# An earlier root, a later compressed branch and moved skip products in a kernel of two transformer blocks

## The chip, the cores and the metric

The kernel runs on one core of a Trainium2 chip (trn2). The metric is the device time of one execution in microseconds (us). The engines are TensorE (PE; PEld are its weight loads), VectorE (DVE), ScalarE (ACT), GpSimd (POOL) and SyncE (SP), which issues the loads of the weights.

## The reference

The input is a sequence of 256 tokens with 1024 features in fp32. The first block has four layers, each a mixer, an MLP with a squared relu and a gate:

```python
for i in range(DEPTH):                # 4
    h = rmsnorm(x, g[0]); kind = i % 3
    ...                               # 0: diff_attention, 1: nsa_attention, 2: forgetting_attention
    x = x + rmsnorm(y, g[1])
    y = sqrelu_mlp(rmsnorm(x, g[2]), mlp_w1[i], mlp_w2[i])
    x = x + rmsnorm(y, g[3])
    x = x + sigmoid(x @ ple_gate_w[i]) * (p[i] @ ple_w[i])
```

Layer 0 is a difference of two softmaxes per head, with a bias that depends on the distance of query and key. Its factor comes from four vectors:

```python
lam_full = exp(sum(lf[0] * lf[1])) - exp(sum(lf[2] * lf[3])) + lam_init
a = pr[:, :, 0] - lam_full * pr[:, :, 1]
```

Layer 1 (`nsa_attention`) has three branches per head, mixed by gates: a selected branch and a window branch on all 256 keys, and a compressed branch on 15 averaged blocks of keys, whose masked softmax gives 0 in a row where no block is visible yet:

```python
p_c = masked_softmax(s_c, m_c)        # 15 blocks; m_c: block wholly in the past
o_c = einsum('bgrqn,bngd->bqgrd', p_c, vc)
return gc[..., 0:1] * o_c + gc[..., 1:2] * o_s + gc[..., 2:3] * o_w
```

The second block has two layers. Each has, beside a latent attention, a state-space branch that ends in

```python
y = ssd_chunked_scan(xh, dt, a, bm, cm) + xh * d_skip[:, None]
```

## The kernel before, in words

The kernel is written as one program per engine, with semaphores between them. An engine runs its own program strictly in the order in which it is written, so a waiting instruction holds up all that stands behind it on that engine. No scheduler changes that order.

**Weights.** SP loads weights in pieces of 128x2048 into one of four slots. ACT rounds each to fp32r (`act_hi`, L441), DVE subtracts to get the rest (`dve_lo`, L451), and PE multiplies three times (L468, L469, L470). Most of PE's work is this. Each `act_hi` and `dve_lo` is placed by hand between the other steps of its engine.

**The start of layer 0** (`act_start`, `dve_start`, `act_da`, `pe_da`). ACT squares the input in four pieces (L632), POOL adds (L608) and DVE finishes the sums (`dve_last_squares`, L620 and L622). PE sums them over the partitions (L628). ACT takes the root (`act_std`, L636, which loads a table of functions first), DVE inverts it (L648), PE spreads it over the partitions (L596), and DVE copies it to `st` (L643). `dve_lam` (L1701, L1703) makes the two sums for the factor `lam_full`, `act_lam` (L1673) their exponentials. In the meantime POOL issues the load of 2 MB of bias rows (L1560). `pe_flip` (L1571) reverses these in two halves of four banks each, and `act_flip` (L1577) copies the banks back. The second half uses the banks of the first, so it waits for those copies. `act_exp_ready` (L1807) loads the table for the exponentials ahead of the attention.

**The second attention** (`act_nsa`, `dve_nsa` and their PE program, layer 1). A loop over 16 pairs j runs scores (L1460), turns of the probabilities (`turn`, L2037) and `values` (L2046 to L2048) on PE. DVE adds the bias and sums the rows (`scaled`: L1379, L1384) and takes up the output (`out`: L1390 to L1415). `values(j)` waits for `out(j-1)`. Weights still come in the first seven pairs. The compressed branch lies in pairs 7 to 15. Its scores are on PE at j=7. At j=8 DVE clears and fills `vbd` (L2269 memset, L2307 copies), adds the biases (L2312) and takes the maxima. At j=9 it normalizes, with a mask (L2326). Then PE turns the probabilities and multiplies them (`block_turned` L2023, `block_values` L2028) at j=10 to 15, and DVE adds the results (`added`, L2276).

**The scan** (second block, both layers) runs over four groups g. DVE makes `bounded` (L2843), `inputs` (L2859, L2861 and the skip products L2864) and `weighted` (L2849). PE's products inside a chunk (L2524) wait for `weighted`, and the next strip of weights in `pe_T` (L468) overwrites what `bounded` reads.

Of the kernel before, what the change touches and what calls it, by code (L numbers as in the profile page):

```python
# [16 lines left out]
P = 128  # L17
D = 1024
S = 256
# [119 lines left out]
def build(nc, d, out, stop=None):  # L139
    ctx = ExitStack()  # L140
    with ctx:
# [152 lines left out]
        s_ca = sem("s_ca")  # L294
        s_stl = sem("s_stl")
# [1071 lines left out]
        def dve_attention(E, n, kind, table, wide=64, strips=None, deep=16, tail=None, middle=None):  # L1367
# [53 lines left out]
            for j in range(n):  # L1421
# [4 lines left out]
                if j < deep and j + 1 < n and (strips is not None or j + 2 < n):  # L1426
                    scaled(j + 1)
                if j >= deep and j + 2 < n:
                    scaled(j + 2)
                if j:  # L1430
                    out(j - 1)
# [129 lines left out]

        def pe_flip(E, half):

            if half:
                E.eng.wait_ge(s_mixa, E.next(s_mixa))
            else:
                E.eng.wait_ge(s_const, E.next(s_const, n_const))
                E.eng.wait_ge(s_rows, E.next(s_rows, 16))
            for b in range(4):
                at = 8 * half + 2 * b  # L1570
                nc.tensor.matmul(ps[:, 2 + b, :], flip[:, :], bias[:, at:at + 2, :].rearrange("p h k -> p (h k)"), start=True, stop=True).then_inc(s_tp, E.adds(s_tp))  # L1571

        def act_flip(E, half):
            for b in range(4):
# [66 lines left out]
        def act_start(E, gcol):  # L1641
# [21 lines left out]
            act_hi_half(E, 1)  # L1663
            E.eng.wait_ge(s_tp, E.next(s_tp))
            nc.scalar.activation(g2[:, 0:n2], ps[:, 3, 0:n2], ACT.Copy)
            for b in range(4):
                act_square(E, b, xT[:, 2 * b:2 * b + 2, :], s_qd)
            act_hi(E)
            act_hi(E)
# [5 lines left out]
        def dve_start(E, gcol):  # L1675
# [18 lines left out]
            dve_lo(E)  # L1694
# [53 lines left out]
        def pe_da(E, layer):  # L1748
# [11 lines left out]
            E.eng.wait_ge(s_st, E.next(s_st))  # L1760
# [23 lines left out]
        def act_da(E, layer):  # L1784
# [5 lines left out]
            act_std(E, DC, 3)  # L1790
# [4 lines left out]
            if layer == 0:  # L1795
                act_flip(E, 0)
# [154 lines left out]
        vcs = view(ar, 12544, [P, 4, 64])  # L1951
# [27 lines left out]
        def pe_nsa(E):  # L1979
# [90 lines left out]
            for j in range(16):  # L2070
# [6 lines left out]
                if j in (0, 2, 4, 5, 6):  # L2077
                    if j == 4:
                        E.eng.wait_ge(s_kv, 1)
                    elif j:  # L2080
                        evicted({2: "q1", 5: "q3", 6: "kwin"}[j])
                    blk = pe_block(E, S, DC)
                    pe_strip(E, "v" if j == 6 else "q", 7, 0, blk)
# [8 lines left out]
                if j in (0, 2, 4, 5, 6):  # L2092
                    pe_strip(E, "v" if j == 6 else "q", 7, 1, blk, s_km if j == 5 else s_mm)
                elif j == 15:
                    E.eng.wait_ge(s_ca, 3)
                    for b in range(2):
                        pe_turn_bank(E, b, orow)
# [8 lines left out]
                if j == 10:  # L2106
                    E.eng.wait_ge(s_cp, 1)
                    block_turned(0)
                elif j == 11:
                    E.eng.wait_ge(s_cc, 1)  # L2110
                    E.eng.wait_ge(s_vb, 1)
                    block_values(0)
                elif j == 12:
                    E.eng.wait_ge(s_ca, 1)
                    block_values(1)
                elif j == 13:
                    E.eng.wait_ge(s_ca, 2)
                    block_turned(1)
                elif j == 14:
                    E.eng.wait_ge(s_cc, 2)  # L2120
                    block_values(0)
                elif j == 15:
                    block_values(1)
            values(15)
            E.skip(s_kd, 3)
# [34 lines left out]
        def act_nsa(E):  # L2160
# [39 lines left out]
            def between(j):  # L2200
# [16 lines left out]
                elif j in (10, 13):  # L2217
                    E.eng.wait_ge(s_ct, {10: 1, 13: 2}[j])
# [4 lines left out]
            act_turn(E)  # L2223

# [5 lines left out]
        def dve_nsa(E):  # L2230
# [48 lines left out]
            def between(j):  # L2279
# [10 lines left out]
                elif j == 3:  # L2290
# [5 lines left out]
                    nc.vector.tensor_copy(vcs[0:NCMP], ps[0:NCMP, 7, S:].rearrange("p (g n) -> p g n", g=4)).then_inc(s_kv, 1)  # L2296
                if 0 < j < 8:
                    dve_lo(E)
                if j == 5:
                    dve_rooted(E, 7)  # L2300
                elif j == 7:
                    nc.vector.memset(pc[:, :, :, NCMP:], 0.0)
                    nc.vector.memset(pc[:, 0:2, :, 7:NCMP], NEG)
                elif j == 8:
                    step(nc.vector.memset, vbd, 0.0)
                    for h in range(4):
                        last = nc.vector.tensor_copy(vbd[32 * h:32 * h + NCMP, :, h, :], vcs[0:NCMP])  # L2307
                    last.then_inc(s_vb, 1)
# [9 lines left out]
                elif j == 9:  # L2318
# [5 lines left out]
                    for q in range(NT):  # L2324
                        x = pc[:, 2 * q:2 * q + 2, :, 0:NCMP]
                        last = nc.vector.tensor_tensor(x, x, cmaskv[:, q, 0:NCMP].unsqueeze(1).unsqueeze(1).to_broadcast([P, 2, 8, NCMP]), ALU.mult)  # L2326
                    last.then_inc(s_d, E.adds(s_d))
                    E.eng.wait_ge(s_d, E.sofar(s_d))
                    nc.vector.tensor_tensor(p15, p15, csm.unsqueeze(3).to_broadcast([P, 4, 8, NCMP]), ALU.mult).then_inc(s_cp, 1)
                elif j in (11, 12, 14, 15):  # L2330
                    added({11: 0, 12: 1, 14: 2, 15: 3}[j])
            dve_attention(E, 16, "nsa", True, strips=between, deep=8)
# [451 lines left out]
        def dve_ssd(E, layer):  # L2784
# [72 lines left out]
            def inputs(g):  # L2857
# [3 lines left out]
                nc.vector.tensor_tensor(xdw[:, :, :], xdt[:, 0], col(2, g), ALU.mult).then_inc(s_xd, 1)  # L2861
                for q in range(NT):
# [6 lines left out]
            for g in range(4):  # L2869
                bounded(g, 0)  # L2870
                E.eng.wait_ge(s_xs, xs0 + 2 * g + 2)
                if g:
                    gated(g - 1, 1)
                    inputs(g)
                    dve_lo(E)
# [3 lines left out]
                else:  # L2879
                    inputs(0)  # L2880
                    weighted(0, 0)
                    dve_lo(E)
                    bounded(0, 1)
# [557 lines left out]
        def _(eng):  # L3441
            E = Track(eng)
            pool_start(E)
            for layer in range(DEPTH):
                pool_added(E, 3)
                pool_added(E, 3)
# [23 lines left out]
        def _(eng):  # L3470
# [3 lines left out]
            act_lam(E)  # L3474
# [19 lines left out]
        def _(eng):  # L3494
            E = Track(eng)
            dve_start(E, g1(0, 0))
            dve_lam(E)
            for layer in range(DEPTH):
                if layer % 3 == 0:
                    lamL[0] = layer // 3  # L3500
                    dve_rstd(E)
                    dve_score_root(E)
                    dve_lo(E)
                    dve_spread(E, 3)
                    dve_strip(E, "k", 0, 1)
                    dve_lo(E)
                    if layer == 0:
# [45 lines left out]
```

## Time and profile before

| | |
|---|---|
| median of 3 runs | 2962.04 us (2955.81 to 2965.88) |
| the profiled execution | 2954.48 us, span 2952.5 us |
| PE busy | 2902.1 us, 98% of the span |
| DVE busy, ACT busy | 2144.8 us, 1532.8 us |
| chain that ended last | PE 88%, DVE 7%, ACT 4% |
| mean granted TensorE clock | 0.989 |

Times in the timelines are us from the start of the span. A row of waits names the waiting engine and line, what it waited for, and the sum, number and longest of the waits. The granted clock is the share of full speed that TensorE was given: 1.00 is 2.4 GHz, near 0.5 is 1.2 GHz.

### The profile page before, as it was taken

To read this page: it belongs to the slowest core of one execution; us is meant where nothing else is said; L and a number is where in the kernel's file an instruction comes from. 1 tells how busy PE (TensorE), PEld (TensorE's weight loads), DVE (VectorE), ACT (ScalarE), POOL (GpSimd) and SP (SyncE) were. 2 spreads that over 40 slices of the span, in tenths; PEclk is the share of its full clock that TensorE was granted. 3 is DMA by queue.
4 is the path that set the end of the run, shared out by engine and by line. 5 is a ranking of instruction groups with operands and counts; after the bars stand their busy time and mean duration, and the time that the engine had idled before them with its cause. 6 is when DMAs were issued, how large, how long until landed. Compare 5 with 4: busy or idle time off the path is not lost.

```text
span 2952.5 us, 44382 instructions
## 1 busy us (share of the span) xinstructions
PE 2902.1 (98%) x18654; PEld 2612.4 (88%) x18654; DVE 2144.8 (73%) x2568; ACT 1532.8 (52%) x2081; POOL 50.6 (2%) x38
## 2 busy tenths in 40 slices
PE   8999998999999999999999999999999999999999
PEld 7888997888988899888988989998888898999988
DVE  5777776676757776776877886658778779765776
ACT  5643565544654356644544845645444466455543
POOL 0000000000000000000100000000000000000000
PEclk9999998999999999999999999999999999999999
DMA  7355451465545654465565544535546544443553
GB/s 241 126 183 198 142 170 55 143 203 175 158 140 172 200 164 140 154 204 192 179 196 159 172 128 148 157 115 191 194 159 210 179 157 137 149 137 125 185 186 114
DMA packets 383191, 482.46 MB, mean 163 GB/s; under 512 B 33201, under 2 KB 330335, under 8 KB 382992
## 3 DMA queue, kind: packets, MB, share of 16 engines
q1 hardware_dynamic: 381832, 477.22, 50.1%
q8 instruction: 148, 2.42, 0.4%
q0 software_dynamic: 560, 2.13, 0.2%
q14 instruction: 51, 0.42, 0.0%
q10 hardware_dynamic: 600, 0.27, 0.0%
HBM read 478.47 MB, written 1.08 MB: 162 GB/s over the span
## 4 chain that ended last, share of the span: by engine, by line
PE 88%; DVE 7%; ACT 4%; issue 2%; POOL 0%; DMA 0%; ACTq 0%; DVEq 0%
PE ps L468 18%; PE ps L470 17%; PE ps L469 17%; PE ps L510 17%; PE ps L514 9%; DVE wl L451 2%; ACT wh L441 2%; PE ps L1460 1%; PE ps L2524 1%; PE ps L781 1%; PE ps L1265 0%; DVE ar L1379 0%; PE ps L2952 0%; PE ps L548 0%; DVE sm L1384 0%
## 5 line engine op out<-in xcount | busy, mean ns | idle before, releaser
L451 DVE TENSOR_TENSOR wl<-raw,wh 128x2048 fp32r<-128x2048 f32 (+1 forms) x462 | 1036.1, 2246 | 352.4 <-ACT wh L441 352.1
L441 ACT ACTIVATE wh<-raw 128x2048 fp32r<-128x2048 f32 (+1 forms) x462 | 860.0, 1874 | 436.0 <-PE ps L510 215.8
L510 PE MATMUL ps<-ahl,wh 128*128 128x512 f32 x2176 | 562.0, 393 | 0.1
L468 PE MATMUL ps<-ahl,wh 128*128 128x256 f32 x1848 | 534.4, 289 | 4.0 <-DVE ar L2843 2.8
L469 PE MATMUL ps<-ahl,wh 128*128 128x256 f32 x1848 | 525.6, 284 | 0.0
L470 PE MATMUL ps<-ahl,wl 128*128 128x256 f32 x1848 | 525.6, 284 | 0.0
L510 PEld LDWEIGHTS ps<-ahl,wh 128*128 128x128 f32 x2176 | 390.5, 189 | 69.3 <-issue 1.3
L468 PEld LDWEIGHTS ps<-ahl,wh 128*128 128x128 f32 x1848 | 357.4, 193 | 12.1 <-issue 5.5
L468 PE MATMUL ps<-wh,ar_r 128*128 128x512 f32 (+1 forms) x944 | 365.0, 387 | 1.2 <-DVE ar_r L1163 1.2
L470 PE MATMUL ps<-wh,ar_r 128*128 128x512 f32 (+1 forms) x944 | 363.8, 385 | 0.0
L469 PE MATMUL ps<-wl,ar_r 128*128 128x512 f32 (+1 forms) x944 | 363.8, 385 | 0.0
L469 PEld LDWEIGHTS ps<-ahl,wh 128*128 128x128 f32 x1848 | 357.5, 193 | 0.3 <-issue 0.2
L470 PEld LDWEIGHTS ps<-ahl,wl 128*128 128x128 f32 x1848 | 357.1, 193 | 0.0
L514 PEld LDWEIGHTS ps<-ahl,wl 128*128 128x128 f32 x2176 | 297.0, 190 | 21.4
L514 PE MATMUL ps<-ahl,wl 128*128 128x256 f32 x2176 | 304.3, 282 | 0.0
L893 ACT ACTIVATE ar_r<-ar 128x512 fp32r<-128x512 f32 x64 | 40.2, 631 | 346.7 <-DVE ar L909 346.7
L468 PEld LDWEIGHTS ps<-wh,ar_r 128*128 128x128 f32 (+1 forms) x944 | 175.4, 186 | 38.7 <-DVE ar_r L1163 2.4
L470 PEld LDWEIGHTS ps<-wh,ar_r 128*128 128x128 f32 (+1 forms) x944 | 175.4, 186 | 36.2
L469 PEld LDWEIGHTS ps<-wl,ar_r 128*128 128x128 f32 (+1 forms) x944 | 175.5, 186 | 35.7
L468 PE MATMUL ps<-wh,ahl 128*128 128x512 f32 (+2 forms) x496 | 171.7, 346 | 2.8 <-issue 1.8
L470 PE MATMUL ps<-wh,ahl 128*128 128x512 f32 (+2 forms) x496 | 168.0, 339 | 0.0
L469 PE MATMUL ps<-wl,ahl 128*128 128x512 f32 (+2 forms) x496 | 168.0, 339 | 0.0
(431 smaller groups left out, 3862.3 us busy)
## 6 DMA issues: line engine op xcount, KB each, us to landing
raw<-in_ffn_w SPq DMA_DIRECT2D x264, 512.0 KB, 4.5
raw<-in_mlp_w SPq DMA_DIRECT2D x256, 512.0 KB, 4.4
raw<-in_w_in SPq DMA_DIRECT2D x124, 512.0 KB, 4.6
raw<-in_da_w_in SPq DMA_DIRECT2D x48, 512.0 KB, 5.0
raw<-in_ple_gate_w SPq DMA_DIRECT2D x32, 512.0 KB, 4.3
raw<-in_w_ssd_out SPq DMA_DIRECT2D x32, 512.0 KB, 4.4
raw<-in_fox_w_in SPq DMA_DIRECT2D x24, 512.0 KB, 4.8
raw<-in_nsa_w_in SPq DMA_DIRECT2D x20, 512.0 KB, 4.9
```

The lines of the kernel that those rows point to most:

```text
L441: nc.scalar.activation(wh[:, slot, 0:sizes[n]], raw[:, slot, 0:sizes[n]], ACT.Copy).then_inc(s_hi, E.adds(s_hi))
L451: nc.vector.tensor_tensor(wl[:, slot, 0:sizes[n]], raw[:, slot, 0:sizes[n]], wh[:, slot, 0:sizes[n]].bitcast(F32), ALU.subtract).then_inc( ...
L468: nc.tensor.matmul(o, wa, xa, start=start, stop=False)
L469: nc.tensor.matmul(o, wa, xb, start=False, stop=False)
L470: return nc.tensor.matmul(o, wb, xa, start=False, stop=stop)
L510: last = nc.tensor.matmul(o, a[:, k, c], ahl[:, k].rearrange("p a t -> p (a t)"), start=k == 0, stop=k == DC - 1)
L514: nc.tensor.matmul(o[:, 0:S], b[:, k, c], ah[:, k], start=False, stop=False)
L781: last = nc.tensor.transpose(o, orow[:, q, c * P:(c + 1) * P], ident[:, :])
L893: nc.scalar.activation(hh[:, u % 3], rr[:, u % 2], ACT.Square).then_inc(s_hh, E.adds(s_hh))
L1460: return nc.tensor.matmul(o, qk[lo, j % 8, 0, qs], keys_of(j)[lo, keys], start=not fox, stop=True)
L2524: last = nc.tensor.matmul(ps[:, 5 + q, 64 * h:64 * h + 64], ee[:, q, h, :], xdt[:, q, h, :], start=True, stop=True)
```

## The change

It has three independent places.

**First block.** ACT's root stands before the last of the first roundings, and DVE's sums come ahead of a rounding. The exponentials for `lam_full` move on ACT from the start to just before the flips. `pe_flip` takes the banks in the order 0, 2, 3, 1, and only bank 1 of the numbering (the fourth taken) waits for `st`.

```diff
 act_start:
+            for b in range(3):
+                act_square(E, b, xT[:, 2 * b:2 * b + 2, :], s_qd)
             E.eng.wait_ge(s_tp, E.next(s_tp))
             nc.scalar.activation(g2[:, 0:n2], ps[:, 3, 0:n2], ACT.Copy)
-            for b in range(4):
-                act_square(E, b, xT[:, 2 * b:2 * b + 2, :], s_qd)
+            act_square(E, 3, xT[:, 6:8, :], s_qd)
             act_hi(E)
+            act_std(E, DC, 3)
             act_hi(E)
 dve_start:
-            dve_lo(E)
             dve_last_squares(E)
             dve_lo(E)
 pe_flip:
-            for b in range(4):
+            for b in FLIPS[half]:        # (0, 2, 3, 1), (0, 1, 2, 3)
                 at = 8 * half + 2 * b
+                if half == 0 and b == 1:
+                    E.eng.wait_ge(s_st, E.next(s_st))
 act_da:
             act_strip(E, "v", 0, 6)
             if layer == 0:
+                act_lam(E)
                 act_flip(E, 0)
```

ACT's program from the squares to the flips of the first half, before and in the change (`g` is the copied gains, `sm` holds small vectors, `wh` the rounded weights):

```order
L632 ACTIVATE ar<-xT 128x512 x4
L441 ACTIVATE wh<-raw 128x2048 x2
L1673 ACTIVATE sm<-sm 128x4
L636 ACT_TABLE_LOAD
L636 ACTIVATE sm<-ps,sm 128x2
L1224 ACTIVATE ar<-ps 128x2x256
L441 ACTIVATE wh<-raw 128x2048 x2
L1221 ACTIVATE ar<-ps,sm 128x256 x2
L441 ACTIVATE wh<-raw 128x2048
L1577 ACTIVATE ar<-ps 128x512 x4
L1807 ACT_TABLE_LOAD
```

```order
L633 ACTIVATE ar<-xT 128x512
L442 ACTIVATE wh<-raw 128x2048
L637 ACT_TABLE_LOAD
L637 ACTIVATE sm<-ps,sm 128x2
L442 ACTIVATE wh<-raw 128x2048
L1225 ACTIVATE ar<-ps 128x2x256
L442 ACTIVATE wh<-raw 128x2048 x2
L1222 ACTIVATE ar<-ps,sm 128x256 x2
L442 ACTIVATE wh<-raw 128x2048
L1682 ACT_TABLE_LOAD
L1682 ACTIVATE sm<-sm 128x4
L1584 ACTIVATE ar<-ps 128x512 x4
```

The root (its table load and 128x2) now stands behind one rounding of weights, the exponentials of 128x4 with a table load of their own stand right ahead of the flips, and the load that followed the flips is gone.

**Second attention.** `vbd` is cleared and filled on POOL, which waits for `out(7)`; DVE loses these five instructions. The mask of the probabilities (two products of 128x240) becomes a mask of the row factor (one of 128x32). At j=9 and j=10 DVE runs `out(j-1)` before `scaled(j+2)`. The products of the compressed branch move one pair later on PE, so that the last of them and the turn of two output banks stand behind `values(15)`. At j=6 PE's `turn` moves ahead of the wait for the window keys.

```diff
 PE, loop over j:
-                if j == 10:
+                if j == 11:
                     E.eng.wait_ge(s_cp, 1)
+                    E.eng.wait_ge(s_vb, 1)
                     block_turned(0)
...
-                elif j == 15:
-                    block_values(1)
             values(15)
+            E.eng.wait_ge(s_ca, 3)
+            block_values(1)
+            for b in range(2):
+                pe_turn_bank(E, b, orow)
+        def pool_nsa(E):
+            E.eng.wait_ge(s_od, 16)
+            nc.gpsimd.memset(vbd, 0.0).then_inc(s_vz, 1)
+            E.eng.wait_ge(s_vz, 1)
+            for h in range(4):
+                last = nc.gpsimd.tensor_copy(vbd[32 * h:32 * h + NCMP, :, h, :], vcs[0:NCMP])
+            last.then_inc(s_vb, 1)
 DVE, between and dve_attention:
-                    step(nc.vector.memset, vbd, 0.0)
-                    for h in range(4):
-                        last = nc.vector.tensor_copy(vbd[32 * h:32 * h + NCMP, :, h, :], vcs[0:NCMP])
-                    last.then_inc(s_vb, 1)
-                    for q in range(NT):
-                        x = pc[:, 2 * q:2 * q + 2, :, 0:NCMP]
-                        last = nc.vector.tensor_tensor(x, x, cmaskv[...], ALU.mult)
+                    step(nc.vector.tensor_tensor, csm.rearrange(...), csm.rearrange(...),
+                         cmaskv[:, :, 0:1].unsqueeze(3).to_broadcast([P, NT, 2, 8]), ALU.mult)
-                elif j in (11, 12, 14, 15):
-                    added({11: 0, 12: 1, 14: 2, 15: 3}[j])
-            dve_attention(E, 16, "nsa", True, strips=between, deep=8)
+                elif j in (12, 13, 15):
+                    added({12: 0, 13: 1, 15: 2}[j])
+            dve_attention(E, 16, "nsa", True, strips=between, deep=8, ahead=(1, 9, 10))
+            added(3)
```

DVE's program from the end of `out(7)` over pairs 8 and 9, before and in the change (`ps` is PSUM, `yT` the output):

```order
L1415 TENSOR_TENSOR yT<-ps,sm 128x2x2x64
L2269 MEMSET ar 128x1024
L2307 COPY ar<-ar 15x4x64 x4
L2312 SCALAR_TENSOR_TENSOR ar<-ps,sm,ar 128x8x7 x2
L2312 SCALAR_TENSOR_TENSOR ar<-ps,sm,ar 128x8x15 x2
L2269 TENSOR_REDUCE ar<-ar 128x32
L2317 TENSOR_TENSOR ar<-ar 128x4x8x15
L1379 SCALAR_TENSOR_TENSOR ar<-ps,sm,ar 128x2x128
L1379 SCALAR_TENSOR_TENSOR ar<-ps,sm,ar 128x2x256
L1384 TENSOR_REDUCE sm<-ar 128x2 x2
L1390 RECIPROCAL sm<-sm 128x4
L1396 TENSOR_TENSOR sm<-sm 128x4
```

```order
L1416 TENSOR_TENSOR yT<-ps,sm 128x2x2x64
L2332 SCALAR_TENSOR_TENSOR ar<-ps,sm,ar 128x8x7 x2
L2332 SCALAR_TENSOR_TENSOR ar<-ps,sm,ar 128x8x15 x2
L2293 TENSOR_REDUCE ar<-ar 128x32
L2337 TENSOR_TENSOR ar<-ar 128x4x8x15
L1391 RECIPROCAL sm<-sm 128x4
L1397 TENSOR_TENSOR sm<-sm 128x4
L1412 TENSOR_TENSOR ar<-ps,sm 128x256
L1414 TENSOR_TENSOR yT<-yT,ar 128x2x2x64
L1380 SCALAR_TENSOR_TENSOR ar<-ps,sm,ar 128x2x128
L1380 SCALAR_TENSOR_TENSOR ar<-ps,sm,ar 128x2x256
L1385 TENSOR_REDUCE sm<-ar 128x2 x2
```

The memset and the copies are gone from between `out(7)` and the biases, and the rows of `out(8)` (128x4 twice, then 128x256 twice) stand ahead of those of `scaled(11)`, which were ahead of them.

**Scan.** The skip products become a step of their own, `skipped(g)`. For g=0 it stands behind `bounded(0, 1)` and the rounding rest; for the other groups the order is as it was.

```diff
                 else:
                     inputs(0)
                     weighted(0, 0)
+                    bounded(0, 1)
                     dve_lo(E)
-                    bounded(0, 1)
+                    skipped(0)
                     weighted(0, 1)
```

DVE's program at the first group of the first scan, before and in the change:

```order
L2859 TENSOR_TENSOR ar<-ar 128x512 x2
L2861 TENSOR_TENSOR ar<-ar 128x512
L2864 TENSOR_TENSOR ar<-ar,sm 128x512 x2
L2849 TENSOR_TENSOR ar<-ar,ps 128x1024
L451 TENSOR_TENSOR wl<-raw,wh 128x2048
L2843 TENSOR_TENSOR ar<-ps,ar 128x512 x2
L2849 TENSOR_TENSOR ar<-ar,ps 128x1024
```

```order
L2877 TENSOR_TENSOR ar<-ar 128x512 x2
L2879 TENSOR_TENSOR ar<-ar 128x512
L2867 TENSOR_TENSOR ar<-ar,ps 128x1024
L2861 TENSOR_TENSOR ar<-ps,ar 128x512 x2
L452 TENSOR_TENSOR wl<-raw,wh 128x2048
L2884 TENSOR_TENSOR ar<-ar,sm 128x512 x2
L2867 TENSOR_TENSOR ar<-ar,ps 128x1024
```

The products of `ar` and `sm` (two of 128x512, the skips) move from ahead of the first `weighted` (128x1024) to behind `bounded(0, 1)` and the 128x2048 of the weights.

## Rows read from the trace of the kernel before

**Rows 1.** The page, first part: busy time, share of the span and instructions of TensorE.

```profile
PE 2902.1 (98%) x18654; PEld 2612.4 (88%) x18654; DVE 2144.8 (73%) x2568; ACT 1532.8 (52%) x2081; POOL 50.6 (2%) x38
```

**Rows 2.** Waits of PE in 0 to 60 us: us in total, times, longest us.

```profile
PE ps L628 <- DVE ar L622: 1.9, 1, 1.9
PE ps L596 <- DVE sm L648: 1.4, 1, 1.4
PE ps L1571 <- DVE st L643: 1.2, 1, 1.2
```

**Rows 3.** Timeline of ACT, 16 to 48 us: start us, us, instruction xcount [idle before <-releaser].

```profile
29.65 0.20 ACT L1673 ACTIVATE sm<-sm 128x4 f32<-128x4 f32 x1 [4.61 <-DVE sm L1703]
29.87 1.28 ACT L636 ACT_TABLE_LOAD   x1
31.16 0.26 ACT L636 ACTIVATE sm<-ps,sm 128x2 f32<-128x2 f32 x1
36.90 1.91 ACT L441 ACTIVATE wh<-raw 128x2048 fp32r<-128x2048 f32 x1 [0.38 <-DMA raw<-in_da_w_in]
38.72 2.04 ACT L1577 ACTIVATE ar<-ps 128x512 f32<-128x512 f32 x4
40.78 1.28 ACT L1807 ACT_TABLE_LOAD   x1
```

**Rows 4.** Timeline of DVE, 22 to 40 us.

```profile
23.27 2.29 DVE L451 TENSOR_TENSOR wl<-raw,wh 128x2048 fp32r<-128x2048 f32 x1 [5.32 <-ACT wh L441]
```

**Rows 5.** Timeline of PE, 44 to 48 us: the second half of the flips.

```profile
45.72 2.74 PE L1571 MATMUL ps<-ar 128*128 128x512 f32 x6
```

**Rows 6.** Timeline of POOL, 14 to 24 us: the issue of the bias rows' load.

```profile
16.79 1.20 POOL L1560 DMA_DIRECT2D ar<-bias_rows  x1 [4.74 <-DMA bias_rows<-ar]
```

**Rows 7.** DMA issues in 0 to 60 us: instruction xcount, KB each, median us to landing.

```profile
ar<-bias_rows POOLq DMA_DIRECT2D x1, 2048.0 KB, 14.0
```

**Rows 8.** Timeline of PE in the second attention: the two matmuls behind the longest waits.

```profile
457.36 0.39 PE L468 MATMUL ps<-wh,ahl 128*128 128x256 f32 x1 [1.08 <-ACT ar L2142]
490.35 0.66 PE L2046 MATMUL ps<-ar 128*128 128x64 f32 x2 [4.98 <-DVE yT L1413]
```

**Rows 9.** Windows: engines' busy time (instructions), then granted clock, DMA share, GB/s.

```profile
470.00:481.00 11.00, 10.10 (x50) 7.96 (x50) 6.03 (x11) 5.12 (x18) 0.00 (x0) 0.53 0.31 97
487.00:498.00 11.00, 7.65 (x38) 6.69 (x39) 9.55 (x24) 6.37 (x20) 0.00 (x0) 0.53 0.00 0
```

**Rows 10.** Timeline of DVE, 476 to 520 us.

```profile
479.11 1.14 DVE L1379 SCALAR_TENSOR_TENSOR ar<-ps,sm,ar 128x256 f32<-128x256 f32 x2 [4.59 <-PE ps L2037]
482.20 0.91 DVE L2269 MEMSET ar<- 128x1024 f32 x1 [0.16 <-issue]
483.15 1.17 DVE L2307 COPY ar<-ar 15x256 f32<-15x256 f32 x4
487.99 1.01 DVE L1384 TENSOR_REDUCE sm<-ar 128x2 f32<-128x256 f32 x2
491.43 0.73 DVE L2326 TENSOR_TENSOR ar<-ar,sm 128x240 f32<-128x240 f32 x2
497.19 1.14 DVE L1379 SCALAR_TENSOR_TENSOR ar<-ps,sm,ar 128x256 f32<-128x256 f32 x2 [1.04 <-PE ps L2037]
500.62 0.69 DVE L2276 TENSOR_TENSOR yT<-yT,ps 128x512 f32<-128x512 f32 x1
```

**Rows 11.** Waits of PE in the first scan, 1700 to 1745 us.

```profile
PE ps L468 <- DVE ar L2843: 1.4, 1, 1.4
PE ps L2524 <- DVE ar L2849: 0.8, 2, 0.6
```

**Rows 12.** Timeline of DVE in the first scan, 1706 to 1728 us.

```profile
1712.33 1.29 DVE L2864 TENSOR_TENSOR ar<-ar,sm 128x512 f32<-128x512 f32 x2
1719.27 1.22 DVE L2849 TENSOR_TENSOR ar<-ar,ps 128x1024 f32<-128x1024 f32 x1 [1.12 <-ACT ar L2700]
```

**Rows 13.** Source L608: POOL's sums; duration ns min/median/max, first and last start us, forms.

```profile
L608 POOL TENSOR_TENSOR ar<-ar x28: 1279/1296/5537, 20.5 to 2766.8; 128x512 f32<-128x512 f32 x28
```

## What the change should do to the time

> **What bounds the kernel now.** I read the page first, then TensorE's waits by stretch, then the timelines of the engine that ended each wait. TensorE (PE) is busy 98% of the span [rows 1], so work taken off another engine is worth nothing by itself. Time can be won only where PE stands, or where it runs at a lower clock. The three places of the change are such places. At the start of layer 0, PE waits 1.9, 1.4 and 1.2 us, one behind the other, for sums, the inverted root and its spread copy [rows 2]. In the second attention it waits 5.0 us for DVE's output step up to 490.35 us, and 1.1 us for ACT's copies of the keys up to 457.36 [rows 8]. From 487 to 498 us, a stretch that begins within the first of these waits, the granted clock is 0.53, that is 1.2 GHz; it is as low from 470 to 481 us [rows 9]. In the scan it waits 1.4 us for `bounded` and 0.8 us for `weighted` [rows 11].
>
> **First block.** A rounding rest of 2.29 us [rows 4] no longer stands ahead of DVE's last sums, so these end about 2 us earlier, more than the 1.9 us that PE waits for them. The root's chain on ACT (load 1.28 us, root 0.26 us [rows 3]) then starts with PE's sums, where before it came behind the 0.20 us of the exponentials for `lam_full`, which had waited 4.61 us for DVE [rows 3]. So the second wait goes too. The third goes because three of four flips no longer need the copy. One new limit has to be looked at: the flips need the bias rows, issued at 16.79 us [rows 6] and landed 14.0 us later [rows 7], so at 30.8 us. The flips began before behind the third wait, and would now begin some 4.5 us earlier, at about 32. The rows are there by then, with about 1 us to spare.
>
> What is late next is ACT. The second half of the flips began at 45.72 us [rows 5], and without the waits would begin at 45.72 − (1.9 + 1.4 + 1.2) = 41.2. It needs the copies of the first half. ACT gets to them behind a rounding that began at 36.90 us, itself held 0.38 us by a landing, and that ended when the copies began, at 38.72 [rows 3]. I take it that this rounding stays, since the weights land when they land. The moved exponentials now stand there: a table load of 1.28 us, 0.20 us for the four numbers, then the copies of 2.04 us [rows 3]. That gives 38.72 + 1.28 + 0.20 + 2.04 = 42.24. **Gain 45.72 − 42.24 = 3.5 us.** The load costs nothing in all, since the one that stood behind the flips, at 40.78 [rows 3], goes; it only moved ahead of them. DVE's sums for `lam_full` come later but stay off this path, being 0.4 us each or less by their size. Upper bound: all three waits, 4.5. Lower bound: one more rounding of 1.91 us [rows 3] is late in front of the flips, 1.6.
>
> The trace has the first function after a table load start 0.01 us behind it (29.87 + 1.28 against 31.16 [rows 3]). The Trainium skill, in "ScalarE: Activation LUTs", section "What ACT_TABLE_LOAD costs", gives 1283 ns for the load and about 1380 ns of drain on top for each switch. By that the copies would end at 43.6, the first block would give 2.1, and the sum below would be 9.8 in place of 11.2. The trace shows the 1.28 and no drain after it, so I keep to the row.
>
> **Second attention.** At pair 6, a turn now fills part of the wait of 1.1 us [rows 8]: between 0 and 1.1, and I take 0.6. At pair 8, DVE loses the memset and copies: from 482.20 us to 483.15 + 1.17 = 484.32 [rows 10], so 2.1 us. The mask falls from 0.73 us [rows 10] to one product of a small tile; the row before shows no such product of this kind, so between 0.4 (if the one costs as much as one of the two) and 0.73, and I take 0.5. The reordering lets `out(8)` start before `scaled(11)`, that is 1.14 + 1.01 = 2.15 us earlier [rows 10]. Together `out(8)` ends 4.3 us earlier, and of PE's wait of 5.0 us 0.7 is left. Not all of that lasts, since the reordering removes no work: DVE still does it two pairs on. What lasts is what DVE no longer does (2.1 + 0.5) and the 1.04 us in which it stood for PE's turn at 497.19 [rows 10], since PE is there sooner. That makes 3.7.
>
> Given back is the tail. The last `block_values` and the turn of two banks, which stood ahead of the last `values`, now stand behind them, and so does one `added` of 0.69 us [rows 10]. PE had waits before `values(15)` that this work partly filled. I bound the price between one `added` (0.7) and three times that, and take 1.4, the `added` and as much for PE's part. Without the clock: 0.6 + 3.7 − 1.4 = 2.9 us.
>
> The clock comes on top. In the stretch from 487 to 498 us PE was busy 7.65 us at 0.53 [rows 9]; at full speed that is 4.05, so 3.6 less. The clock fell while PE stood for 5.0 us [rows 8, 9]; with 0.7 left there it may not fall. But DVE is busy 9.55 of those 11 us [rows 9], so PE's speed counts only where the two wait for each other, and I take 1.6, a bit under half. **Gain 4.5 us.** Bounds: 6.5 with all of the 3.6. Below, POOL's work runs beside DVE's; if DVE is slowed by as much as it gave away (2.1), 0.8 is left.
>
> The moved work must not be late itself. POOL starts at `out(7)`, around 482.2. The first product with `vbd` needs the normalized probabilities, whose last step followed the masks at 491.43 + 0.73, so about 492 before and, a pair later in the change, not much sooner. That is a cover of some 10 us. POOL took 1.30 us (median) for a sum of 128x512 [rows 13]; the memset is two of that size, and the four copies are smaller, so at most 6 × 1.30 = 7.8 us. It costs nothing.
>
> **Scan.** The two skip products (1.29 us [rows 12]) go from ahead of `weighted(0,0)`, and the rounding rest of about 2.3 us (as in [rows 4]) from ahead of `bounded(0,1)`. `bounded` then ends some 3.5 us earlier, and PE's 1.4 us [rows 11] goes. The shorter of the two waits for `weighted`, 0.8 − 0.6 = 0.2, goes with it, since PE's own work before it then sets its start. That is 1.6 per layer, 3.2 for the two. What is late next: the skips now stand before `weighted(0,1)`, but DVE stood 1.12 us before that one for ACT [rows 12], which comes earlier with `bounded`, so the step is still ahead of its old time by about 1 us. If everything behind hangs on it, 0.95 per layer is left, 1.9 in all. Upper bound: 1.4 + 0.8 per layer, 4.4. **Gain 3.2 us.**
>
> **Sum.** 3.5 + 4.5 + 3.2 = 11.2 us. The profiled execution took 2954.5, so its counterpart is 2943.3. The median of the runs shown is 2962.0, 7.6 us above that execution, so the forecast for a median is 2962.0 − 11.2 = **2950.8 us**. What this kernel's measurement can tell from no change is about 0.3%, or 8.9 us.
>
> **The rivals.** *Given back (0.22).* DVE is slowed beside POOL so that the second attention gives 0.8, and the flips wait for one more rounding so that the first block gives 1.6; with 3.2 of the scan that is 5.6, 2956.4 us. For it: DVE is the busier engine in the second attention. Against: POOL's span is short. *The first block does nothing (0.12).* Landings could hold ACT's roundings, and PE with them; the waits would only change their names. Then 7.7, 2954.3 us. For it: the 0.38 us that a landing held ACT [rows 3]; against: PE's three waits name DVE. *The clock stays at 2.4 GHz in both stretches (0.10).* In the one from 470 to 481 us PE was busy 10.10 us, and DVE then stood 4.59 us for PE's turn [rows 10]. With these and all of the 3.6, the second attention gives 2.9 + 3.6 + 4.6 = 11.1 and the sum is 17.8, 2944.2 us. Against: the change alters only 1.1 us of waiting ahead of 470.
>
> *POOL is late, slower than before (0.04).* POOL's sums have a longest of 5.54 us [rows 13], so something stretches them. If the six sizes above all cost that, `vbd` takes 33.2 us, 23 beyond its cover of 10, and PE stands for them: 2950.8 + 23 = 2974 us. It decides from 10 us of POOL's time on, and makes the kernel slower by over 0.3% from about 10 + 11.2 + 8.9 = 30 us. Against: the median is 1.30, and one instruction of 28 is no rule. The Trainium skill, "GPSIMD Engine Reference", section "Specifications", says that GpSimd's way to SBUF is shared with VectorE and contended when VectorE reads two SBUF inputs; its opening calls GpSimd the wrong choice for elementwise work. The longest row agrees with the first; the median says that it is no rule here.
>
> **How the numbers follow.** The forecast has 0.52. The range reaches from 2943 (the clock's case, a little inside) to 2958 (all lower bounds: 1.6 + 0.8 + 1.9 = 4.3, so 2957.7). Faster by over 0.3% are the forecast and the clock's case: 0.62. Within 0.3% are the first two rivals: 0.34. Slower: 0.04.
>
> **What would show it.** In the profile of the changed kernel, PE's waits before 60 us would be one of about 1 us, for ACT's flip copies, in place of three. The second flip would start near 42.2. The wait of 5.0 us in the second attention would be under 1, and the granted clock between 487 and 498 tells the rest. POOL should end `vbd` before 490. The wait for `bounded` should be missing in both scans. A wait for POOL, a long wait behind the ACT table load, or a clock that falls for longer, would prove me wrong.

## The result and the profile after

Six runs of the changed kernel lay between 2940.33 and 2945.31 us, median 2943.20. The kernel before, in six runs, had a median of 2956.74. The ratio is 0.9950 (95% interval 0.9938 to 0.9961), so the change makes the kernel faster by 11 to 18 us. The profiled executions differ by 14.4 us in their spans: 2952.5 before, 2938.1 after.

The page of the changed kernel, first part, then two of PE's waits in its first 60 us, read as in [rows 2]:

```profile
PE 2897.0 (99%) x18654; PEld 2608.3 (89%) x18654; DVE 2142.2 (73%) x2562; ACT 1532.3 (52%) x2081; POOL 53.3 (2%) x43
```

```profile
PE ps L1578 <- ACT ar L1584: 1.4, 1, 1.4
PE ps L1266 <- ACT ar L1326: 0.5, 1, 0.5
```

The three waits of [rows 2] are gone; the one of 0.5 us was there before too. A new one of 1.4 us stands in front of the second half of the flips (L1578; the lines of the change lie 1 to 22 higher than those of before). ACT's timeline shows why, as in [rows 3]; its last row is the copies of the flips:

```profile
21.70 1.28 ACT L637 ACT_TABLE_LOAD   x1
25.18 0.26 ACT L637 ACTIVATE sm<-ps,sm 128x2 f32<-128x2 f32 x1 [2.20 <-PE ps L629]
...
36.95 1.91 ACT L442 ACTIVATE wh<-raw 128x2048 fp32r<-128x2048 f32 x1 [0.39 <-DMA raw<-in_da_w_in]
38.88 1.28 ACT L1682 ACT_TABLE_LOAD   x1
40.18 0.20 ACT L1682 ACTIVATE sm<-sm 128x4 f32<-128x4 f32 x1
40.29 2.04 ACT L1584 ACTIVATE ar<-ps 128x512 f32<-128x512 f32 x4
```

On PE, the second half of the flips, which was at 45.72 us [rows 5]:

```profile
42.38 3.70 PE L1578 MATMUL ps<-ar 128*128 128x512 f32 x8 [1.38 <-ACT ar L1584]
```

The first half of the flips starts at 31.58 us, 0.15 us after PE's last work before it. The bias rows that it needs were issued at 17.14 us and landed at 31.45.

In the second attention, PE's wait of 4.98 us at 490.35 [rows 8] has become 0.5 at 481.05. A wait for ACT's copy stands behind it:

```profile
481.05 0.41 PE L2057 MATMUL ps<-ar 128*128 128x64 f32 x2 [0.48 <-DVE yT L1414]
...
485.74 1.12 PE L2048 MATMUL ps<-ident,ar 128*128 128x128 f32 x6 [2.30 <-ACT ar L1331]
...
510.83 0.47 PE L469 MATMUL ps<-wh,ahl 128*128 128x512 f32 x1 [1.23 <-issue]
```

The last of these rows is the first matmul of the output projection. I call a stretch in which the granted clock is 0.50, so 1.2 GHz, a half-clock stretch. Two windows that hold one each, in the columns of [rows 9], then POOL's new work:

```profile
469.00:476.00 7.00, 7.00 (x35) 5.25 (x35) 3.17 (x7) 4.03 (x15) 0.00 (x0) 0.51 0.46 148
...
486.00:493.00 7.00, 7.00 (x36) 6.02 (x35) 5.54 (x13) 4.55 (x17) 0.00 (x0) 0.51 0.00 0
```

```profile
477.29 0.95 POOL L2243 MEMSET ar<- 128x1024 f32 x1 [118.42 <-DVE yT L1416]
478.30 2.09 POOL L2246 COPY ar<-ar 15x256 f32<-15x256 f32 x4
```

On DVE, two products of 128x32 now stand where one of them and the two masks of 0.73 us [rows 10] stood:

```profile
483.99 0.43 DVE L2293 TENSOR_TENSOR ar<-ar,sm 128x32 f32<-128x32 f32 x2
```

In the first scan, the wait of 1.4 us of [rows 11] is gone. One wait for `weighted` and a short one for ACT are left:

```profile
PE ps L2542 <- DVE ar L2867: 0.6, 1, 0.6
PE ps L2531 <- ACT yT L2750: 0.3, 1, 0.3
```

**Where the 14.4 us came from.** Both kernels have the same number of PE instructions, so I compared the start of the same instruction in both profiles at places where their order is the same. Times are those of the kernel before; the lead of the changed kernel is in us:

| up to | lead | what lies before it |
|---|---|---|
| 60 us | 3.23 | the flips |
| 452 us | 2.89 | half-clock stretches at the start of layer 1 that fall otherwise |
| 600 us | 8.31 | the second attention, 5.4 |
| 1690 us | 8.25 | |
| 1740 us | 9.89 | the first scan, 1.64 |
| 1870 us | 11.37 | a half-clock stretch at 1842 us that the changed kernel doesn't have, 1.5 |
| 2460 us | 11.35 | |
| 2500 us | 13.03 | the second scan, 1.68 |
| 2620 us | 14.47 | a half-clock stretch at 2603 us that it doesn't have, 1.5 |
| the end | 14.45 | |

Within the second attention the lead is 3.5 us at 470 us, 0.6 more than at 452. That goes with the turn at pair 6: PE's wait for the copied keys went from 1.08 [rows 8] to 0.27 us.

The stretch at 1842 us, in the windows of the kernel before, follows 24 products of the norm with `ones` on PE, in which PE stood for nothing:

```profile
1839.03 2.74 PE L2623 MATMUL ps<-ones,ar 128*128 128x1 f32 x24
```

```profile
1842.35:1845.75 3.40, 3.40 (x18) 3.40 (x18) 1.31 (x2) 1.88 (x4) 0.00 (x0) 0.50 0.12 29
```

In the changed kernel the same products run from 1829.16 us, and no stretch follows:

```profile
1829.16 2.74 PE L2641 MATMUL ps<-ones,ar 128*128 128x1 f32 x24
```

```profile
1832.00:1836.00 4.00, 4.00 (x34) 3.93 (x34) 1.78 (x2) 2.16 (x5) 0.00 (x0) 1.00 0.32 85
```

### The profile page after: what moved, and what is told of

The parts are those of the page before. It is cut to its first block, busy times and chain, and to the rows that moved or that the text cites. A ratio compares the mean times of both kernels' runs of the same rounds, so it can differ in the third digit from the quotient of the medians.

```text
span 2938.1 us, 44382 instructions
## 1 busy us (share of the span) xinstructions
PE 2897.0 (99%) x18654; PEld 2608.3 (89%) x18654; DVE 2142.2 (73%) x2562; ACT 1532.3 (52%) x2081; POOL 53.3 (2%) x43
## 3 DMA queue, kind: packets, MB, share of 16 engines
HBM read 478.47 MB, written 1.08 MB: 163 GB/s over the span
## 4 chain that ended last, share of the span: by engine, by line
PE 88%; DVE 7%; ACT 3%; issue 1%; DMA 1%; POOL 0%; ACTq 0%; DVEq 0%; SPq 0%
PE ps L469 18%; PE ps L471 17%; PE ps L470 17%; PE ps L511 17%; PE ps L515 9%; DVE wl L452 2%; ACT wh L442 1%; PE ps L1463 1%; PE ps L2542 1%; PE ps L782 1%; PE ps L1266 0%; ACT ar L1326 0%; DMA raw<-in_da_w_in 0%; PE ps L2974 0%; PE ps L549 0%
```

## The experiments

**One part alone (e1, e2, e3), and the kernel before again (e4).** Each is the kernel before with the hunks of one place of the change, so their diffs are the three pieces shown ahead of the prediction; e4 has no edit. Each ratio in this section is to runs of the kernel before on the same chip. The sets e1 to e4, e5 to e8, e9 to e11 and e12 ran on four chips, so between sets the ratios are the fairer measure, and medians only a second one.

> The kernel before with the change of the first block alone. Theory (the three places add up, each by what PE no longer waits): 3.2 us faster, ratio 0.9989, the second flip near 42.4 us behind a wait of 1.4 us for ACT's copies. Rival (the first block's gain is given back later, since layer 1 begins with another fall of the clock near 388 us): under 2 us, ratio above 0.9993.

> The kernel before with the change of the second attention alone. Theory: 5.4 us faster there, ratio 0.9982, the half-clock stretches at 470 and 487 us shortened from 10.2 to 6.8 us. Rival (the shorter half-clock stretches are chance or come from the first block's earlier start, not from this place): 3 us, ratio 0.9990, with stretches of 10.2 us.

> The kernel before with the change of the scan alone. Theory: 1.65 us in each scan, 3.3 in all, ratio 0.9989, and the short half-clock stretches near 1842 and 2603 us come or go as in any run of before. Rival (moving the skip products also takes these two stretches away): 6.3 us, ratio 0.9979, neither stretch in the profile.

> The kernel before, unchanged, as a measure of what differs between executions of one kernel. Theory (the short half-clock stretches outside the changed places are chance): ratio 1.000, and the set of half-clock stretches outside 470 to 498 us differs from that of the first profile, with 1.5 us of span for each of 3.4 us. Rival (they are fixed by the program): the same stretches at the same places, span within 0.5 us of 2952.5.

Measured, against 35 runs of the kernel before (median 2957.48):

| run | median us | ratio | 95% interval |
|---|---|---|---|
| e1, first block | 2955.26 | 0.9995 | 0.9986 to 1.0003 |
| e2, second attention | 2953.72 | 0.9985 | 0.9976 to 0.9995 |
| e3, scan | 2951.35 | 0.9977 | 0.9968 to 0.9985 |
| e4, before again | 2958.24 | 1.0005 | 0.9997 to 1.0014 |

The three add up to 0.9957, which the interval of the whole change holds. The first block alone is within what can be told from no change; its interval holds the 3.2 expected. Its profile shows the gain at 60 us (3.5). The interval of e2 holds its theory and its rival. Its half-clock stretches were 10.2 and 6.8 us long, so one was shortened and one not. But e1 and e4, with the old attention, have 6.8 and 6.8, so these lengths vary between executions and do not speak for or against the change. In its profile PE takes 60.7 us from `values(5)` to the output projection, where the first profile of before has 65.2: 4.5 us from this place by itself. The scan is outside what I had expected: its interval leaves out the 3.3 us of the waits and holds the rival's 6.3. Neither of the stretches at 1842 and 2603 is in e3's profile: against the first profile of before, the scans give 1.65 and 1.72 us and the two missing stretches 1.5 each, 6.4 in all. Its span is only 3.1 us shorter, since it has two stretches at the end of the second attention (510.7 and 521.0 us) that the first profile of before lacks.

The unchanged kernel's second profile (e4) is 5.0 us longer in its span than its first. It has the two stretches again, at 1844 (there 6.8 us long) and 2608, and three at places where the first had none:

```profile
509.10:512.50 3.40, 3.40 (x14) 2.94 (x14) 1.88 (x5) 0.44 (x1) 0.00 (x0) 0.50 0.00 0
519.30:522.70 3.40, 3.40 (x10) 2.62 (x9) 0.14 (x1) 0.00 (x0) 0.00 (x0) 0.50 0.00 0
1720.80:1724.20 3.40, 3.40 (x18) 3.40 (x17) 3.05 (x4) 2.65 (x3) 0.00 (x0) 0.50 0.67 234
```

So e4's theory was half right: the set of stretches does differ between executions of one kernel. But the two stretches I had taken for chance came again. A single profile is no measure of a change of this size.

**The changed kernel with one thing undone (e5 to e8).** e5 is the changed kernel itself. e6 puts `vbd` back on DVE:

```diff
                 elif j == 8:
+                    step(nc.vector.memset, vbd, 0.0)
+                    for h in range(4):
+                        last = nc.vector.tensor_copy(vbd[32 * h:32 * h + NCMP, :, h, :], vcs[0:NCMP])
+                    last.then_inc(s_vb, 1)
                     E.eng.wait_ge(s_cs, 1)
...
-                if layer == 1:
-                    pool_nsa(E)
```

e7 takes the order of `out` and `scaled` back, e8 moves the exponentials for `lam_full`, with a semaphore of their own:

```diff
-            dve_attention(E, 16, "nsa", True, strips=between, deep=8, ahead=(1, 9, 10))
+            dve_attention(E, 16, "nsa", True, strips=between, deep=8, ahead=())
```

```diff
             if layer == 0:
-                act_lam(E)
-                act_flip(E, 0)
+                act_flip(E, 0, 2)
+                act_lam(E)
```

> The changed kernel, unchanged, on the chip of the next three, as their base and to see what differs between executions. Theory (the three places give 12 us, and 3 us of the 14.4 between the two first profiles are short half-clock stretches after the 24 one-column products near 1830 and 2588 us, which come in some executions only): ratio 0.9950 to 0.9960. Rival (moving the skip products keeps those two stretches away for good): none of them in this profile either, ratio 0.9945 to 0.9952.

> The changed kernel with the clearing and filling of vbd back on DVE, ahead of the biases. Theory (DVE's chain sets the pace there, POOL's copy is hidden): PE's wait for out(8) grows from 0.5 to 2.6 us, 2 us slower than the changed kernel, ratio 0.0007 higher. Rival (DVE has room there, since PE's waits for ACT and its lower clock set the pace): less than 0.5 us.

> The changed kernel with out(8) and out(9) again behind scaled(11) and scaled(12). Theory (the order counts by itself): a wait of 2.2 to 2.7 us for out(8) comes back in front of values(9), 1 to 2 us slower than the changed kernel. Rival (the order only exchanged a wait for DVE against the new wait of 2.3 us for ACT's copy, L1331): that wait goes in exchange, 0.5 us or less in all.

> The changed kernel with the exponentials for lam_full behind the copies of the first flips, where the table load of before stood. Theory (the second flips wait for the table load and the exponentials, 1.28 + 0.20 us): they start 1.4 us earlier, near 41.0 us, the wait of 1.4 us for ACT goes, 1.4 us faster than the changed kernel. Rival (the load is only exchanged: it then holds ACT's next step, L1225, and the attention starts no earlier): below 0.3 us.

| run | median us | ratio to before | 95% interval |
|---|---|---|---|
| e5, changed again | 2943.29 | 0.9945 | 0.9931 to 0.9958 |
| e6, vbd on DVE | 2945.53 | 0.9951 | 0.9937 to 0.9966 |
| e7, old order of out | 2942.41 | 0.9944 | 0.9930 to 0.9957 |
| e8, lam_full late | 2941.13 | 0.9939 | 0.9925 to 0.9953 |

e5 gave the ratio of the first measurement again within its interval, and one of the two late stretches, those behind the scans (here at 1834 us). So they do not stay away for good. Its interval overlaps both forecasts. The intervals of e5 to e8 overlap one another, so what tells these apart is the profile of each, with the median as a second sign. e6: the wait for `out(8)` is back at 2.9 us, and PE takes 62.0 us from `values(5)` to the output projection, where e5 and the first profile of the change take 60.5 and 59.8. That is 1.5 to 2.2 us for the theory's 2, and the median is 2.2 us higher. The waits of PE in e6, then in e7, in the second attention:

```profile
PE ps L2057 <- DVE yT L1414: 4.1, 3, 2.9
```

```profile
PE ps L2057 <- DVE yT L1414: 3.8, 3, 2.6
PE ps L2057 <- DVE yT L1416: 2.7, 2, 2.3
PE ps L2057 <- ACT ar L1331: 1.8, 2, 0.9
```

In e7 the wait for DVE came back as expected (2.6 us), and the wait of 2.3 us for ACT's copy is missing in its rows. The median is 0.9 us lower than e5's, not 1 to 2 higher. The profile of e7 has both half-clock stretches at 10.2 us and is 61.9 us long there, but e12, with the same order and stretches of e5's lengths, has e5's length, 60.4 and 60.5. That fits the rival: the order exchanged one wait for another.

e8 moved the second flips as expected; on PE and ACT:

```profile
40.94 3.70 PE L1579 MATMUL ps<-ar 128*128 128x512 f32 x8 [0.28 <-ACT ar L1585]
```

```profile
38.85 2.03 ACT L1585 ACTIVATE ar<-ps 128x512 f32<-128x512 f32 x4
40.91 1.28 ACT L1683 ACT_TABLE_LOAD   x1
```

PE's wait falls from 1.38 to 0.28 us, and against e5's profile PE is 1.4 us ahead at 60 us and still at 380. The median is 2.2 us lower than e5's. So the table load and the exponentials ahead of the flips did cost what stands in the rows, and can be had back.

**The scan undone, the pairs undone, the wait filled (e9 to e11).** e9 is the change without its hunks in the scan. e10 puts the compressed branch's products back into pairs 10 to 15 (PE, ACT's copies and DVE's `added` together). e11 fills PE's wait:

```diff
+                if j == 11:
+                    for _ in range(10):
+                        nc.tensor.matmul(ps[:, 3, 0:P], ones[:, :], ones[:, :], start=True, stop=True)
                 turn(j)
```

The products of e11 overwrite scores of one head of pair 13 in PSUM, so that head's output is computed from other numbers, by the same instructions.

> The changed kernel with the scan as before. Theory (the 1.65 us per scan also move what follows, so that the 24 one-column products near 1830 and 2588 us no longer pull the clock down: 1.5 us more in each layer): both half-clock stretches come back, 6 us slower than the changed kernel, ratio near 0.9965. Rival (those stretches are chance): 3.3 us slower, ratio near 0.9956, and none or one of the two stretches.

> The changed kernel with the products of the compressed branch in their old pairs (10 to 15). Theory (a pair later they find their probabilities ready): PE waits 2.6 us at pair 10 for the normalized probabilities, about 1.5 us slower than the changed kernel. Rival (the later pair only moves work into the tail, where block_values and the turn of two banks cost 1.4 us): the new wait takes the place of the 2.3 us for ACT's copy and the tail is shorter, 0 to 1.4 us faster than the changed kernel.

> The changed kernel with 10 products of ones by ones (20 matmuls of 128x128, results unused) in PE's wait for ACT's copy at pair 11. Theory (the clock falls at 486 us because PE stands 2.3 us there): the granted clock stays 1.00 from 480 to 500 us, DVE's wait of 1.6 us for the turn goes, 1 to 2 us faster than the changed kernel. Rival (the clock falls for the thin stretch as a whole, not for this wait): the stretch stays, 0 to 0.5 us slower.

| run | median us | ratio to before | 95% interval |
|---|---|---|---|
| e9, without the scan's part | 2946.16 | 0.9955 | 0.9943 to 0.9967 |
| e10, old pairs | 2946.90 | 0.9954 | 0.9941 to 0.9966 |
| e11, filled wait | 2942.34 | 0.9946 | 0.9933 to 0.9960 |

e9 is 2.9 us above e5 by the medians and 0.0010, or 3.0 us, by the ratios, which is the rival's 3.3 rather than the theory's 6; its interval holds both ratios. In its profile the wait of 1.4 us for `bounded` is back, one of the two late stretches is back (2594.6 us), and a stretch within the scan itself came too:

```profile
1710.60:1714.00 3.40, 3.40 (x18) 3.40 (x17) 2.42 (x3) 3.39 (x4) 0.00 (x0) 0.50 0.86 291
```

Against e5's profile the two scans cost 2.6 us (with that stretch) and 1.7, and each of the two profiles has one late stretch, so these cancel. So e9 does not price the late stretches.

Counting over all profiles: with the old scan (the kernel before twice, e1, e2, e9) a half-clock stretch follows the 24 products in 8 of 10 places, and one lies within a scan in 4 of 10. With the new scan (the changed kernel twice, e3, e6, e7, e8, e10, e11, e12) it is 3 of 18 and 0 of 18. The same traces show what the late stretches go with. For each of the 28 places I take the time from the end of the half-clock stretch ahead of the scan (near 1620 and 2380 us) to the first of the 24 products:

| time in us | places | followed by a stretch |
|---|---|---|
| 209.8 to 210.5 | 15, all with the new scan | 0 |
| 211.0 to 213.0 | 8 with the old scan, 3 with the new | 11 |
| 213.6 and 213.9 | 2 with the old scan, and a stretch within it | 0 |

In the two first profiles it is 1839.03 - 1627.31 = 211.7 us before and 1829.16 - 1619.39 = 209.8 in the change. In all 28 places, then, the time at which the products begin tells whether a stretch follows. The new scan brings them forward by the 1.65 us that PE no longer waits, in 15 of 18 places to the side without a stretch. So the late stretches go with timing. No run was made to test this, and why the limits lie where they do is not shown.

e10: PE waits for the normalized probabilities, as the theory said, and the wait of 2.3 us for ACT's copy is gone in exchange, as the rival said. The wait, then the window in which its output projection begins:

```profile
PE ps L2034 <- DVE ar L2348: 2.6, 1, 2.6
```

```profile
512.90:519.70 6.80, 6.09 (x14) 4.79 (x15) 1.27 (x4) 0.00 (x0) 0.00 (x0) 0.50 0.00 1
```

The medians put it 3.6 us above e5, the ratios 0.0009 or 2.7 us; one of its five runs, at 2941.44, is as fast as the changed kernel. From `values(5)` to the output projection its profile has 61.4 us, where the four profiles with the new pairs and stretches of the same lengths (e2, e5, e9, e12) have 60.4 to 60.7; the rest of the 3.7 us that it loses to e5's between 452 and 600 us lies in its last stretch. With the old pairs, a half-clock stretch lies at the end of the attention in e1, e3, e4 and e10, and only the first profile of before has none; with the new pairs none of the nine profiles has one. So moving the branch a pair later is worth a wait and, in most executions, that stretch.

e11: with PE kept at work, the granted clock stayed at 2.4 GHz from 480.8 us on, as the theory said. Window, then PE:

```profile
480.80:500.00 19.20, 16.53 (x137) 13.86 (x135) 17.99 (x46) 12.60 (x45) 2.92 (x5) 1.00 0.00 1
```

```profile
487.48 2.50 PE L2104 MATMUL ps<-ones 128*128 128x128 f32 x20
...
495.27 0.84 PE L2048 MATMUL ps<-ident,ar 128*128 128x128 f32 x6 [1.86 <-ACT ar L1331]
```

Each of the other 13 profiles has a half-clock stretch here. So this one hangs on PE's wait, as far as one profile can show it. The time did not follow beyond what the runs can tell: the stage is 59.3 us long, 0.4 to 1.1 less than in the changed kernel, and a wait of 1.86 us for ACT came one pair on. The medians of e11 and e5 differ by less than either's own runs.

**Both cheap edits (e12).** The change with e7's and e8's edits.

> The changed kernel with both edits that cost nothing or gave time: the exponentials behind the copies of the first flips, and out(8), out(9) in their old order. Theory (the first gives 1.4 us, the second nothing either way): 1.4 us faster than the changed kernel, ratio 0.9935 to 0.9945. Rival (the old order costs the 2 us that its one profile showed between the start and the end of the second attention): 0.6 us slower than the changed kernel, ratio 0.9945 to 0.9952.

Measured: median 2941.35 us, ratio 0.9942 (0.9928 to 0.9955), 1.9 us below e5. The ratios differ by 0.0003, or 0.9 us. In its profile no wait for the flips is left, but this says little: the first half of the flips started at 33.19 us there, 1.6 us later than in the change, and the second half at 42.37, as in the change. The interval holds the theory and the rival. e8 and e12 have the lowest medians of all, and are the versions I would keep, though by less than the runs can separate.

## Why the prediction was right or wrong

**The direction was right, the size too small, and the step that failed is the scan's "Gain 3.2 us".** I forecast 11.2 us; measured are 14.8 by the ratio (11 to 18) and 13.5 by the medians. The forecast time of 2950.8 us was set on the median of three runs, 2962.04. Six runs gave 2956.74 and later sets of 9 to 35 runs 2957.5 to 2959.9. Some 2 to 5 us of the distance between 2950.8 and 2943.2 is this level, the rest is the size. In the first two profiles the size is 14.4: the scan gave about 3 us more than forecast, the second attention 0.9 more, and the first block and the start of layer 1 some 0.6 less. That 2943.2 lies beside the 2944.2 of the clock's rival is chance: that rival keeps the clock up in both stretches of the second attention, and the windows there show 0.51.

**First block: right, but for the time to spare.** Forecast were 3.5 us, a second half of the flips at 42.24 us, and ACT as what is late next. The profile shows 3.23, 42.38, and a wait of 1.4 us for ACT's copies. The table load ran 38.88 + 1.28 = 40.16 and the exponentials began at 40.18. Where the Trainium skill's page "ScalarE: Activation LUTs", section "What ACT_TABLE_LOAD costs", adds a drain, this row has none behind the load, as before. The bias rows were to be there "with about 1 us to spare"; they landed 0.13 us before the first flip. In the ten profiles with this part 0.13 to 0.8 us were left, and in four of them PE waited for the landing, by 0.15 us at most. e8 bought the 1.4 us back.

**Second attention: the sum near, the parts not.** Forecast were 4.5 us; the pair of profiles shows 5.4, and five profiles with the whole of this part take 59.8 to 60.7 us from `values(5)` to the output projection, where four of the old one take 65.2 to 66.6. Right were the turn at pair 6 (0.6 forecast and seen), `vbd` (2.1 forecast; 1.5 to 2.2 in e6), the mask (0.5 forecast; 0.73 us became 0.43 - 0.20 = 0.23), that POOL hides `vbd` (0.95 and 2.09 us, done at 480.4, 8.7 us before PE's first product that waits for it), and that the order of `out` lasts for nothing (e7, e12). POOL's work beside DVE slowed nothing that the rows show. DVE's four biases at the same time took 1.17 us, as they do in the timeline of before.

Two steps failed here. The first is **"Given back is the tail"**. I had priced the later pair as a loss of 1.4 us alone. e10 shows the opposite sign: undone, it costs 2.7 to 3.7 us, by a wait of 2.6 us for the normalized probabilities that the old pairs would now have, and by a half-clock stretch at the end. I had not asked when those probabilities are ready for the old place once `out(8)` comes 4 us earlier. The second is **"The clock comes on top"**, with 1.6 us. The clock did not stay up: the stretch that began at 487 us begins at 486 in the change. It is 6.8 us long there in place of 10.2, but three of the four profiles with the old attention have 6.8 too. And e11, which keeps the clock up, shortened the stage by 0.4 to 1.1 us, not 1.6. One term of the wrong sign and one too high partly cancelled, so that the sum is near is luck.

**Scan: the waits right, the clock left out.** Forecast were 3.2 us; the waits gave 1.64 and 1.68. But e3 measured 4.4 to 9.5 us for this part alone, and the first pair of profiles shows 3.0 us in the two stretches that no longer follow the 24 products. A place with PE busy on both sides got no clock term at all, though I had given the second attention one. e9 measured about 3 us for taking this part out again, in a profile in which the late stretches cancel; so between 3 and 7 us is what the runs support. The 3.0 us are a shift in time: PE comes to the products 1.65 us sooner after the stretch ahead, and in 15 of 18 places no stretch follows there. Nothing in the prediction pointed to this, and a later edit that moves the same products can bring the stretches back, as three places show.

**The rivals.** None of them happened as described. POOL's late work needed 10 us to matter and took 3.1. In the first block, landings held PE by 0.15 us at most and ACT's last rounding by 0.39. "Given back" did not happen. The clock's case is answered above.

## What to carry to other kernels

Where TensorE is busy nearly all the time, price a removed wait together with the half-clock stretch that may follow it, and look for it behind the wait as well as in it. Such a stretch can go with the moment at which one-column products come, so an edit that saves 1.65 us can gain or lose 1.5 more at another place. A step that is moved later has to be priced at its old place in the new order: what would it wait for if it stayed. Undoing one part at a time told `vbd`, the order and the pairs apart where their sum in one profile looked as forecast. With effects of 1 to 3 us beside a spread of 5 us between executions, one profile of each kernel is not enough.

## What the runs showed of the hardware

A table load for the root ran at 21.70 us, before ACT's wait of 2.20 us for PE's sums, and the root itself took 0.26 us when the sums came. In the kernel before, the load ran at 29.87 us [rows 3], behind the exponentials for `lam_full`, though PE's sums had ended at 27.3. So a table load in front of a waiting function is not held by that function's wait.

One kernel's executions differ by several us in where the clock is at 1.2 GHz: the two profiles of the kernel before are 5.0 us apart, with the same longest waits in the first scan (1.4 us) and in the second attention (5.0 us). Each of the stretches of 3.4 us in dense work at 1842 and 2603 us cost 1.5 us of the span. A stretch follows the 24 one-column products, in which PE stood for nothing, in 11 of 28 places, and the time at which the products begin tells in which (the table of 28 places).
